# ScalarE's order in the first attention tile: a gate's bank emptied ahead of the head's work, positions 1 to 15

## What is computed

```
z  = RMSNorm(x) @ w_in              # q_a k_a v_a q_b k_b v_b gate_a gate_b
h  = x + (sigmoid(gate_a) * (A @ w_a) + sigmoid(gate_b) * (B @ w_b)) @ w_o
y  = RMSNorm_final(h + PEER(RMSNorm(h)))
```

## Time and profile before

| | us |
|---|---|
| median of 3 runs | 1915.52 |
| lowest, highest | 1913.15, 1916.68 |
| the profiled execution's own time | 1914.36 |
| its span, first to last instruction | 1912.4 |
| PE busy, PEld busy | 1411.9, 644.1 |
| DVE busy, ACT busy | 1215.1, 378.1 |
| POOL busy | 1067.4 |
| moved by DMA | 706.43 MB, mean 369 GB/s |

### The profile page before, as it was taken

One profiled execution on the slowest core, in us unless ns is written; L12 is line 12 of the kernel. 1 busy time (PEld: TensorE's weight loads), 2 busy tenths in 40 slices (PEclk: granted clock), 3 DMA queues, 4 the chain that ended last, 5 costly groups with the idle time before them and its releaser, 6 DMA issues.

```text
span 1912.4 us, 18881 instructions
## 1 busy us (share of the span) xinstructions
PE 1411.9 (74%) x5470; PEld 644.1 (34%) x5470; DVE 1215.1 (64%) x3335; ACT 378.1 (20%) x922; POOL 1067.4 (56%) x1082
## 2 busy tenths in 40 slices
PE   8999978885785779666889575657566566667568
PEld 5444434453342344322234232323232233332112
DVE  1015343267766668666766688788787888898452
ACT  2113433221222222211111111221111122112001
POOL 3010000036665677676656777776777777777773
PEclk9999988987898798877999777888887888878768
DMA  9999995778999899999999999999999999999996
GB/s 326 366 326 359 361 338 195 262 234 311 361 401 396 323 355 405 352 401 398 373 403 358 401 409 409 409 409 410 409 409 409 408 409 407 401 389 409 409 410 254
DMA packets 226135, 706.43 MB, mean 369 GB/s; under 512 B 21152, under 2 KB 46656, under 8 KB 226008
## 3 DMA queue, kind: packets, MB, share of 16 engines
q0 software_dynamic: 166912, 612.40, 83.0%
q1 hardware_dynamic: 59120, 92.82, 13.9%
HBM read 700.65 MB, written 72.61 MB: 404 GB/s over the span
## 4 chain that ended last, share of the span: by engine, by line
DMA 38%; PE 23%; issue 15%; POOL 11%; DVE 10%; ACT 1%; SPq 0%; POOLq 0%; DVEq 0%; ACTq 0%
DMA XS<-in_peer_u_dram,e_all 15%; DMA arena<-in_peer_u_dram,e_all 12%; POOL WR L660 5%; PE bank L947 5%; PE bank L1076 4%; DMA GT<-in_peer_u_dram,e_all 4%; DMA WR<-in_peer_v_dram,arena 4%; PE bank L1059 4%; POOL XS L660 3%; DVE XS L1463 2%; PE bank L1154 2%; POOL arena L660 2%; POOL GT L660 2%; PE bank L1175 1%; PE bank L1196 1%
## 5 line engine op out<-in xcount | busy, mean ns | idle before, releaser
L1059 PE MATMUL bank<-WR,arena 128*64 128x512 f32 x1728 | 515.9, 740 | 263.5 <-DMA WR<-in_peer_v_dram,arena 245.9
L660 POOL DMA_INDIRECT WR<-in_peer_v_dram,arena x432 | 421.8, 976 | 196.7 <-issue 134.0
L660 POOL DMA_INDIRECT XS<-in_peer_u_dram,e_all x258 | 275.0, 1066 | 227.1 <-DVE e_all L1432 79.8
L1059 PEld LDWEIGHTS bank<-WR,arena 128*64 128x64 f32 x1728 | 148.8, 168 | 578.2 <-issue 515.2
L1463 DVE SCALAR_TENSOR_TENSOR XS<-XS,bank 128x1024 f32<-128x1024 f32 x144 | 175.0, 1221 | 86.2 <-DMA XS<-in_peer_u_dram,e_all 82.2
L1463 DVE SCALAR_TENSOR_TENSOR GT<-GT,bank 128x1024 f32<-128x1024 f32 x126 | 152.4, 1220 | 80.9 <-DMA GT<-in_peer_u_dram,e_all 78.1
L1463 DVE SCALAR_TENSOR_TENSOR XS<-XS,GT 128x1024 f32<-128x1024 f32 x114 | 138.3, 1225 | 92.9 <-DMA XS<-in_peer_u_dram,e_all 91.8
L660 POOL DMA_INDIRECT GT<-in_peer_u_dram,e_all x126 | 122.8, 975 | 47.7 <-issue 34.7
L660 POOL DMA_INDIRECT arena<-in_peer_u_dram,e_all x128 | 126.6, 989 | 40.6 <-issue 38.1
L1076 PE MATMUL bank<-WR,XS 128*128 128x512 f32 x256 | 118.3, 617 | 15.3 <-ACT GT L807 14.9
L1463 DVE SCALAR_TENSOR_TENSOR arena<-arena,bank 128x1024 f32<-128x1024 f32 x90 | 109.9, 1221 | 9.2 <-DMA arena<-in_peer_u_dram,e_all 5.9
(11 more groups left out here) (234 smaller groups left out, 2066.8 us busy)
## 6 DMA issues: line engine op xcount, KB each, us to landing
out_dram<-in_cache_a_k_dram POOLq DMA_DIRECT2D x8, 4064.0 KB, 54.1
out_dram<-in_cache_a_v_dram POOLq DMA_DIRECT2D x8, 4064.0 KB, 54.5
WR<-in_w_in_dram SPq DMA_DIRECT2D x8, 2048.0 KB, 25.0
GT<-in_w_peer_q_dram SPq DMA_DIRECT2D x14, 1024.0 KB, 16.2
WR<-in_w_out_dram SPq DMA_DIRECT2D x6, 2048.0 KB, 16.9
WR<-in_peer_v_dram,arena POOLq DMA_INDIRECT x432, 14.4
WR<-in_w_branch_a_dram SPq DMA_DIRECT2D x6, 1024.0 KB, 8.5
WR<-in_w_branch_b_dram SPq DMA_DIRECT2D x6, 1024.0 KB, 12.1
```

The costliest lines, as they stand in the source:

```text
L660: nc.gpsimd.indirect_dma_start(dst, None, table, bass.IndirectOffsetOnAxis(ap=idx, axis=0))\
L1059: last = nc.tensor.matmul(b[c][R * j:R * j + R, :], diag[p // QUAD % 4][:, s % 4, :], V[V_AT[s]][:, c * CHUNK:(c + 1) * CHUNK], start=Fals ...
```

## The change

The key that sorts the pieces of a position for all engines but TensorE now knows the position: where it is not 0, a gate comes at 1, ahead of what stands at 2, that is ahead of the head, `half`, `end`, and of a gate_sum.

```
-def other_order(pieces, beside):
+def other_order(x, pieces, beside):
...
-    return sorted(pieces, key=lambda p: 3 if beside and p[0] in ATT else FIRST.get(p[0], 2))
+    return sorted(pieces, key=lambda p: 3 if beside and p[0] in ATT else 1 if x and p[0] == "gate" else FIRST.get(p[0], 2))
...
-PLAN = [other_order(pieces, beside(x, pieces)) for x, pieces in enumerate(PLAN)]
+PLAN = [other_order(x, pieces, beside(x, pieces)) for x, pieces in enumerate(PLAN)]
```

## The result

| | before | after |
|---|---|---|
| median of 6 runs, us | 1915.32 | 1905.66 |
| lowest, highest | 1911.87, 1917.21 | 1898.07, 1908.00 |
| ratio, 95% interval | | 0.9937, 0.9918 to 0.9956 |
| profiled execution, own time | 1914.36 | 1907.22 |

By the medians the change gains 9.7 us, by the ratio 12 (8 to 16); the forecast was 1904, a gain of 11.4, with a range of 1900 to 1912. Both kernels scatter: in later runs on one chip the kernel before took 1908.13 to 1926.78 over 29 runs, the one after 1896.52 to 1908.90 over 12. The profiled execution of the kernel after, 7.1 us under that of before, is one of its slower ones, so its rows are no mean.

What follows compares the result with a forecast made beforehand. Mostly transfers, but the later gathers start when tile 0 is through, and TensorE's waits for ScalarE to empty banks delay that. 11.7 + 0.6 - 0.9 = 11.4 us gained, forecast 1904 us, range 1900 to 1912.

Steps and rivals of the forecast that it cites:

- Gate 12 starts without a wait: TensorE at gate 12: gate 11's bank is emptied at once, so it runs at about 244.7 to 252, beside VectorE's stall.
- Gate 13 behind gate_sum 2: TensorE at gate 13: waits for gate_sum 2's bank behind head 9's exponent, starting at 254.4, not 264.81: 10.4 us.
- Gate 17 at 283.25 behind keys 5: TensorE at gate 17: waits for gate 16's bank behind head 13's exponent, with keys 5 landing at 274.05; before 294.95.
- sample_soft's 0.6: At sample_soft: VectorE's 1.1 us of waiting, less 0.5 for the delayed exponent of the sink, leaves a gain of 0.6.
- The signs in the profile after: Gate starts, post(0) at 311, first gather near 379, stalls in sample_qk(3) and sample_qk(5), waits for ScalarE down to about 4.
- Rival B: Behind 330 us: the lead is lost later, at a date that didn't move; price all of it, 1915.5; chance 0.11.
- Gates 7 to 11: TensorE there: 3.7 us won at gate 7 is lost at gate 10 to chunk 6, landing at 233.0; no lasting gain.
- The cover that I had counted for it: Before gate 13: a slow start of gate 10 has 2.0 us to spare, 252.4 against 254.4.
- Gates 14 to 17: TensorE up to gate 17: it starts at 283.25 instead of 294.95, a lead of 11.7 us.
- the 2.64 of the upper bound: TensorE's clock: a restart after standing costs 0 to 2.64 us; the sum took 0.9 for gate 17.
- sample_qk(3), which doesn't move: VectorE's products with keys 3 end when they did, so keys 5 are issued by 256.95.
- Rival A: Keys 5's landing sets gate 17: late gives 1911.7, early 1901.3; chance 0.15 for its long end, 0.06 for its short.

Runs made afterwards that it cites:

- only_gate11: Kernel before the change with only gate 11 emptied ahead of its head, the other 14 gates left behind: 1909.08 us, ratio 0.9976.
- after_again: The changed kernel measured once more, unaltered, on the same chip as three other variants: 1903.38 us, ratio 0.9937 to the kernel before.
- early_gates_only: Kernel before the change with only gates 5 to 10 (positions 1 to 6) emptied ahead of the head: 1915.03 us, ratio 0.9993.
- sum_ahead_too: The changed kernel with the three gate_sums emptied ahead of the head as well: 1905.61 us, ratio 0.9955 to the kernel before.

## Why the prediction was right, and where it was off

**The rows of the forecast that hold.** Gate 12 starts without a wait: it did at 245.80 in only_gate11 (forecast 244.7 to 245). Gate 13 behind gate_sum 2: seen twice, 3.75 and 0.80 us. Gate 17 at 283.25 behind keys 5: 282.56 in after_again. sample_soft's 0.6: post(0) gains 0.7 on gate 17 in the profile after (9.04 against 8.38).

**The signs in the profile after.** Most of those that the prediction named did not come there: gate 12 at 251.88 (245), gate 13 at 259.64 (254.4) and gate 17 at 286.57 (283), both without a wait, post(0) at 313.96 (311), the first gather at 381.99 (379), TensorE's waits for a gate's bank 0 (about 4), VectorE's stall 5.95 (9) and none in sample_qk(5). The time is in the range, but in this execution the lead came by another path: chunk 6 held TensorE back, so that keys 3 and 5 were not waited for. The forecast's path is that of after_again.

**The lead passes through.** Rival B was wrong. From the first gather to the end of the own time it takes 1520.7 to 1529.5 us in all 14 profiled executions, while the first gather moves from 371.45 to 405.28. What 380 us shows, the end shows within about 4 us. That is enough against B, and too little to read 3 us out of one execution.

**Gates 7 to 11.** "All of the lead is lost there" was right in sum (early_gates_only, 0.9993) and wrong as a date. 233.0 was the landing of one execution; it was 227.8 to 236.2 in others. In the profile after it came at 236.2, 3 us late, and with the slow clock that it brought (3.64 and 9.11 us for gates 10 and 11, at a granted 0.50 and 0.78) cost gate 12 7 us against the forecast's 244.7. The cover that I had counted for it (until 254.4) was used up: gate 13 came at 259.64, a lead of 5.2 where the forecast had 10.4.

**Gates 14 to 17: a term that was mis-sized.** 11.7 us at gate 17 became 8.4 in the profile after (5.2 from gate 13, and the waits of gates 16 and 17) and 12.4 in after_again (282.56), which then paid 2.8 for the restart: 9.6. I had set 0.9 for it, and 1.85 for the longest wait that gate 17 could have; there it was 4.36. With the 2.64 of the upper bound in its place the sum is 9.7. That this is also the difference of the first medians is no proof: the interval holds 11.4 as well, and in the profile after gate 17 ran at full speed (7.13), the loss lying at gates 10 and 11. Between the gates a wait of 4.36 us cost 2.77, 3.75 cost 1.67, and waits of 0.80 to 2.21 cost nothing but for the one before gate 7 (2.05 to 2.06: 1.67, in three executions). Why that one differs no run shows.

**"sample_qk(3), which doesn't move."** It does: with all copies issued as before, it begins its products between 238.70 and 248.19 in the nine profiles, and keys 5 follow its end.

**Rival A** is the right description of the scatter, with more dates than its one: TensorE came to wait because of chunk 6 in the profile after, chunk 7 in sum_ahead_too, keys 3 in only_gate11 and keys 5 in after_again. Keys 7 were late too (6.33 in the profile after), but no profile shows TensorE paying for it.

**What the cause is.** The argument put the gain down to the stall of 8.9 us in sample_qk(3). The runs show two sources that overlap: the stall (worth 8.4 us by the ratio when four copies are left out and the transfers come in time; that trace is 9.1 ahead at gate 13 already, so the stall was paid at gate 12) and five short waits of the same form (worth 9.8 by themselves). The change reaches both, and collects 10 to 12 of 18.

**What stays open.** Whether the split between gate 11 and the others is even, as the medians have it, or not: each half is known to within about 4 us only. Whether the gates emptied earlier also bring the keys earlier: sample_qk(3) began at 238.70 to 247.61 in the seven profiles with gates 7 to 9 ahead, at 245.22 and 248.19 in the two without, too few to tell. And what sets the landing of chunk 6 from one execution to the next was not tried apart from the copies beside it.

## What to carry to other kernels

In an engine that works in order, put what frees a buffer ahead of what waits for a third engine, even where each wait looks short: here, with the transfers in time, five waits of 0.98 to 2.21 us were worth as much as the one of 8.8 us was with them late. When a lead is to be carried past a stretch in which the queues are full, ask of each transfer in it when it lands, and take the landing of one profile as one draw of several. A stretch whose queues are a quarter idle on the average has no room for a long copy if the next weights are asked for only when they are needed.

## What was not expected of the hardware

- The landing of the same 2 MB load (chunk 6), issued between 196.7 and 198.7 us beside the same copies, took 31.0 to 38.3 us over nine executions. The Trainium skill, "DMA: Bandwidth & Descriptors", section *Issuing engines are not separate DMA queues*, says that transfers of all issuing engines end on the same 16 DMA engines and interleave there. The traces agree: with four of GpSimd's copies moved next to it, a load of 1 MB issued by SyncE takes 31.4 us where it took 9.4. For chunk 6 the copies left out say less: 34.0 and 27.0 us in the two kernels with fewer of them.
- TensorE ran 16 matmuls of 128x512 in 7.1 us, and in 8.80, 9.75, 9.77, 9.90 or 10.03 right behind waits of 2.05 to 9.88 us (granted clock 0.81 at 8.80, 0.72 at 9.77); behind waits of 2.21 and 2.12 it lost nothing (7.11, at 1.00).
